# Expert weights of a two-layer transformer step: one landing buffer each for gate, up and down

## The reference

```python
gates = jnp.einsum('nk,nke->ne', g_w * top_w, jax.nn.one_hot(expert_id, N_EXPERTS, dtype=jnp.float32))
hid = jax.nn.silu(jnp.einsum('nd,edf->nef', x, w1)) * jnp.einsum('nd,edf->nef', x, w3)
out = jnp.einsum('nef,efd->nd', hid * gates[:, :, None].astype(hid.dtype), w2)
```

## Time and profile before

| | us |
|---|---|
| three runs, median | 2075.46 |
| three runs, lowest and highest | 2069.21, 2075.76 |
| the profiled execution, its own time | 2068.9 |
| its span, from first to last instruction | 2067.1 |
| its mean granted TensorE clock | 0.939 of full |

### The profile page before, as it was taken

How to read it: one execution, slowest core, us unless ns; L and a number is a source line. 1 busy time by engine, 2 the same in 40 slices (tenths; PEclk the granted TensorE clock), 3 DMA queues, 4 the chain that set the end, 5 groups by cost and what they waited for, 6 DMA issues and landing times. The chain is left out here.

```text
span 2067.1 us, 28080 instructions
## 1 busy us (share of the span) xinstructions
PE 1827.7 (88%) x11240; PEld 1513.8 (73%) x11240; DVE 1047.9 (51%) x1563; ACT 800.5 (39%) x1085; POOL 256.5 (12%) x242
## 2 busy tenths in 40 slices
PE   6799899999999996899849998989999999848892
PEld 2798555679999983677628975556799999737671
DVE  3322566762323456787672226477522334557784
ACT  2311261663112321677662203516521223227773
POOL 0101510000000000253220033100000000004430
PEclk8799999999999998899958999999999999969996
DMA  9113301312222418898762123021111225249984
GB/s 362 57 60 85 110 27 57 120 50 65 79 62 92 163 72 299 328 353 320 279 252 84 50 68 136 22 102 63 62 62 62 92 72 194 82 158 352 348 317 187
DMA packets 127958, 299.90 MB, mean 145 GB/s; under 512 B 10792, under 2 KB 53352, under 8 KB 119144
## 3 DMA queue, kind: packets, MB, share of 16 engines
q1 hardware_dynamic: 110664, 264.15, 35.2%
q0 software_dynamic: 9792, 20.99, 2.7%
q10 hardware_dynamic: 7392, 13.19, 2.2%
HBM read 283.25 MB, written 29.72 MB: 151 GB/s over the span
## 5 line engine op out<-in xcount | busy, mean ns | idle before, releaser
L1887 PE MATMUL pair<-hT_r,mid_r 128*128 128x320 f32 x768 | 237.3, 309 | 0.0
L1887 PE MATMUL pair<-mid_r,r_r 128*128 128x512 f32 (+1 forms) x528 | 193.9, 367 | 23.7 <-DVE hT_r L1679 23.6
L1887 PE MATMUL pair<-r_r,ring_r 128*128 128x320 f32 x832 | 211.8, 309 | 2.2 <-DVE ring_r L1254 2.2
L1669 DVE TENSOR_TENSOR ring_r<-ring,mid_r 128x2048 fp32r<-128x2048 f32 x68 | 155.7, 2292 | 59.1 <-ACT mid_r L1072 59.0
L1887 PE MATMUL pair<-ysT_r,mid_r 128*128 128x256 f32 (+1 forms) x768 | 172.1, 315 | 14.7 <-issue 9.5
L1887 PE MATMUL pair<-mid_r 128*128 128x320 f32 x576 | 178.9, 311 | 1.6 <-issue 1.6
L1887 PE MATMUL pair<-r_r,mid_r 128*128 128x256 f32 (+2 forms) x576 | 180.2, 313 | 0.0
L1887 PE MATMUL pair<-mid_r,ring_r 128*128 128x320 f32 x576 | 178.0, 309 | 0.0
L1969 PE MATMUL pair<-cst,mid 128*128 128x128 f32 x748 | 119.7, 300 | 64.1 <-DVE mid L1200 32.0
L1969 PEld LDWEIGHTS pair<-cst,mid 128*128 128x128 f32 x748 | 92.6, 153 | 111.3 <-DVE mid L1200 39.7
L1482 DVE TENSOR_TENSOR r<-pair,r 128x640 f32<-128x640 f32 x48 | 39.5, 823 | 252.3 <-PE pair L1887 252.3
(11 more groups left out here) (276 smaller groups left out, 3827.7 us busy)
## 6 DMA issues: line engine op xcount, KB each, us to landing
ring<-in_w_mod SPq DMA_DIRECT2D x23, 2048.0 KB, 8.8
ring<-in_w_gate SPq DMA_DIRECT2D x34, 1024.0 KB, 5.9
ring<-in_w_up SPq DMA_DIRECT2D x34, 1024.0 KB, 8.4
ring<-in_w_down SPq DMA_DIRECT2D x34, 1024.0 KB, 9.4
ring<-in_w_in SPq DMA_DIRECT2D x24, 1024.0 KB, 7.0
ring<-in_w_in SPq DMA_DIRECT2D x8, 2048.0 KB, 10.8
ring<-in_w_branch SPq DMA_DIRECT2D x12, 1024.0 KB, 5.1
ring<-in_w_out SPq DMA_DIRECT2D x8, 1024.0 KB, 5.3
```

Of the source, the lines that this page charges most:

```text
L1669: V.tensor_tensor(w13_parts[s][1][:, own], w13[s][:, own], w13_parts[s][0][:, own], ALU.subtract).then_inc(w13_ready, 1)
L1887: return nc.tensor.matmul(out, lhsT, rhs, start=first, stop=last, skip_group_check=True)
```

## The change

Three landing places take the place of four. Gate lands in 2048 columns of the ring, up in another 2048, down in 2048 columns of `hT`. Both parts of the split go elsewhere: the high parts of gate and up to `mid_r` as before, the remainders to the ring halves where they stood before; the two parts of down go to one copy each in `ysT_r`. SP issues the next load into a landing place when DVE has made the remainder from it. ACT rounds gate, down and up one after another, ahead of the hidden values, and the rounding of down(b) waits for PE's down(b-1), as its parts have one copy now. The core of the diff:

```diff
-        w13 = [view(ring, (1 - s) * 6144, 4096) for s in range(2)]
-        w2s = [view(ring, (1 - s) * 6144 + 4096, 2048) for s in range(2)]
+        gate_land, up_land, down_land = view(ring, 10240, 2048), view(ring, 4096, 2048), view(hT, 3072, 2048)
         w13_parts = [(view(mid_r, s * 4096, 4096), view(ring_r, (1 - s) * 6144, 4096)) for s in range(2)]
-        w2_parts = [(view(ysT_r, s * 2048, 2048), view(ring_r, (1 - s) * 6144 + 4096, 2048)) for s in range(2)]
+        w2_parts = view(ysT_r, 0, 2048), view(ysT_r, 2048, 2048)
...
-                    sp.wait_ge(h_filled, b + 1)
-                    for w, at_, signal in ((w_gate, 0, gate_in), (w_up, 2048, up_in)):
...
+                def load_gate(b):
 
                     e = expert_of(b)
+                    if not isinstance(b, int) or b:
+                        sp.wait_ge(gate_ready, b)
+                    load_up_part(e, w_gate, gate_land, gate_in)
...
+                def load_up(b):
 
                     e = expert_of(b)
+                    if not isinstance(b, int) or b:
+                        sp.wait_ge(up_ready, b)
+                    load_up_part(e, w_up, up_land, up_in)
+
+                def load_down(b):
+
+                    e = expert_of(b)
+                    if not isinstance(b, int) or b:
+                        sp.wait_ge(w2_ready, b)
...
-                load_up(0, 0)
-                await_job(sp, ("mod", mods_of(L) - 1))
-                load_up(1, 1)
-                load_down(0, 0)
...
+                load_gate(0)
+                load_up(0)
+                load_down(0)
+                load_gate(1)
+                load_up(1)
+                load_gate(2)
+                load_up(2)
+                load_gate(3)
+                load_down(1)
+                load_up(3)
                 with sp.Fori(0, n_more) as it:
+                    for s in range(2):
+                        load_gate(it * 2 + (4 + s))
+                        load_down(it * 2 + (2 + s))
+                        load_up(it * 2 + (4 + s))
+                for s in range(2):
+                    load_down(n_more * 2 + (2 + s))
...
+                def round_down(b):
+
+                    act.wait_ge(down_in, b * 16 + 16)
+                    act.wait_ge(y_filled, b + 2)
+                    nc.scalar.copy(w2_parts[0], down_land).then_inc(rounded, 1)
...
                     gate_values(b, s)
                     if not (last and s):
                         round_tokens(b + 1, 1 - s)
-                    round_down(s, rnd)
+                    if not last:
+                        round_gate(b + 2, s)
+                    round_down(b)
+                    if not last:
+                        round_up(b + 2, s)
                     round_hidden(b, s)
                     if not (first and s == 0):
                         store_block(b - 1, 1 - s, rnd - 1 + s)
-                    if not last:
-                        round_up(s, rnd + 1)
...
+                    if not last:
+                        remainder_gate(s, b * 5 + 7)
+                    remainder_down(b * 5 + (8 if not last else 7 if not s else 4))
+                    if last:
+                        remainder_hidden(s, b * 5 + (5 if s else 8))
+                    else:
+                        remainder_hidden(s, b * 5 + 10)
                         remainder_up(s, b * 5 + 9)
...
-                    pe.wait_ge(w13_ready, b * 2 + 2)
+                    pe.wait_ge(gate_ready, b + 1)
+                    pe.wait_ge(up_ready, b + 1)
```

More of the change, by code:

```diff
@@ L469, in bass_hybrid_step @@
         picked = [sem(f"picked{i}") for i in range(TT)]
-        gate_in = [sem(f"gate_in{i}") for i in range(2)]
-        up_in = [sem(f"up_in{i}") for i in range(2)]
-        rounded, w13_ready, w2_ready = sem("rounded"), sem("w13_ready"), sem("w2_ready")
+        gate_in, up_in = sem("gate_in"), sem("up_in")
+        rounded, gate_ready, up_ready, w2_ready = sem("rounded"), sem("gate_ready"), sem("up_ready"), sem("w2_ready")
         hid_turned, down_ready = sem("hid_turned"), sem("down_ready")
-        down_in = [sem(f"down_in{i}") for i in range(2)]
+        down_in = sem("down_in")
         t_filled, t_freed, h_filled, sil_ready, hid_ready, y_filled, y_read = (
@@ L748, in expert_of, with load_up_part @@
                     return sp.value_load(blk_ids[0:1, ds(b, 1)], min_val=0, max_val=NE - 1)
-                def load_up(b, s):
+                def load_up_part(e, w, land, signal):
+                    sp.dma_start(land, w[ds(L * NE + e, 1)].rearrange("a (p k) f -> p (a k f)", p=P)).then_inc(signal, 16)
+                def load_gate(b):
                     e = expert_of(b)
-                    sp.wait_ge(h_filled, b + 1)
-                    for w, at_, signal in ((w_gate, 0, gate_in), (w_up, 2048, up_in)):
-                        sp.dma_start(w13[s][:, at_:at_ + 2048], w[ds(L * NE + e, 1)].rearrange("a (p k) f -> p (a k f)", p=P))\
-                            .then_inc(signal[s], 16)
@@ L1066, in _, with round_gate, round_up @@
                 n_more = act.value_load(pairs_more[0:1], min_val=2, max_val=NB // 2 - 2)
[L1068 to L1077, removed]
+                def round_gate(b, s):
+                    act.wait_ge(gate_in, b * 16 + 16)
+                    nc.scalar.copy(w13_parts[s][0][:, 0:2048], gate_land).then_inc(rounded, 1)
+                def round_up(b, s):
+                    act.wait_ge(up_in, b * 16 + 16)
+                    nc.scalar.copy(w13_parts[s][0][:, 2048:4096], up_land).then_inc(rounded, 1)
+                def round_down(b):
+                    act.wait_ge(down_in, b * 16 + 16)
+                    act.wait_ge(y_filled, b + 2)
+                    nc.scalar.copy(w2_parts[0], down_land).then_inc(rounded, 1)
                 def round_tokens(b, s):
@@ L1102, in _ @@
                     act.wait_ge(h2_stored[i], 16 * ((TT + 1 - i) // 2))
+                round_gate(0, 0)
                 round_up(0, 0)
                 round_tokens(0, 0)
-                round_up(1, 0)
+                round_gate(1, 1)
+                round_up(1, 1)
                 def block_rounds(b, s, rnd, first, last):
@@ L1662, in _, with remainder_gate, remainder_down @@
                 dve.sem_inc(down_ready, 2)
+                def remainder_gate(s, count):
+                    dve.wait_ge(rounded, count)
+                    V.tensor_tensor(w13_parts[s][1][:, 0:2048], gate_land, w13_parts[s][0][:, 0:2048], ALU.subtract).then_inc(gate_ready, 1)
                 def remainder_up(s, count):
[L1666 to L1671, removed]
                     dve.wait_ge(rounded, count)
-                    V.tensor_tensor(w2_parts[s][1], w2s[s], w2_parts[s][0], ALU.subtract).then_inc(w2_ready, 1)
+                    V.tensor_tensor(w13_parts[s][1][:, 2048:4096], up_land, w13_parts[s][0][:, 2048:4096], ALU.subtract).then_inc(up_ready, 1)
+                def remainder_down(count):
+                    dve.wait_ge(rounded, count)
+                    V.tensor_tensor(w2_parts[1], down_land, w2_parts[0], ALU.subtract).then_inc(w2_ready, 1)
                 def remainder_tokens(s, count):
@@ L1692, in _ @@
                 n_more = dve.value_load(pairs_more[0:1], min_val=1, max_val=NB // 2 - 2)
-                remainder_up(0, 1)
+                remainder_gate(0, 1)
+                remainder_up(0, 2)
                 remainder_tokens(0, 3)
-                remainder_up(1, 4)
+                remainder_gate(1, 4)
+                remainder_up(1, 5)
                 def block_remainders(b, s, last):
@@ L1701, in block_remainders @@
                         remainder_tokens(1 - s, b * 5 + 6)
-                    remainder_down(s, b * 5 + (4 if last and s else 7))
-                    remainder_hidden(s, b * 5 + (5 if last and s else 8))
                     if not last:
+                        remainder_gate(s, b * 5 + 7)
[4 more added lines that the diff above has]
+                        remainder_hidden(s, b * 5 + 10)
                         remainder_up(s, b * 5 + 9)
@@ L2295, in down @@
                             last = three_products(out[:, j * 512:(j + 1) * 512], [x[:, k * P:(k + 1) * P] for x in hid_parts[s]],
-                                                  [x[:, k * D + j * 512:k * D + (j + 1) * 512] for x in w2_parts[s]], k == 0, k == FT - 1)
+                                                  [x[:, k * D + j * 512:k * D + (j + 1) * 512] for x in w2_parts], k == 0, k == FT - 1)
                     last.then_inc(y_filled, 1)
```

14 lines of the change are left out of this document (2 added, 12 removed).

## The result

The changed kernel takes 2113.84 us (median of four runs, 2110.06 to 2121.12), the kernel before, run beside it, 2072.34 us. The ratio is 1.0193, with a 95% interval from 1.0164 to 1.0223: about 40 us slower. The forecast was slower, 2083 us, and its range ended at 2103. The side was right, the forecast size a fifth of what came.

The account below looks back on a forecast made before the run. PE and the DMA engines were both taken as near their limits, neither at it. Steady part +2.3 and tails +5.5 made +7.8 us: 2068.9 became 2076.7, with the runs' median 6.6 higher 2083; range 2061 to 2103.

Parts of the forecast that it names:

- The loop: Up's single landing buffer in the experts: each block's period is the load plus 5.3 us to the next issue, 11.0 us.
- signs that I had named against myself: Profile signs against the forecast: gates 9.4 us apart, ACT waiting for gate or down, down's rounding waiting for PE, E(3) off 871.
- the steady part: Experts' blocks from E(3) to the last: 26 periods of 11.0 us, 286.0 against 283.7, so +2.3 us.
- E(3): Block 3's mark in the experts, where the sum of periods starts; claimed to stay at 871.0 us in layer 0.
- The load in it: Up's load from issue to landing: 5.7 us taken, from 4.9 to 6.6, with one gather or scatter crossing it in full.
- The tail: End of each layer's experts: PE waits 4.75 us for the last down parts, 2.76 more than before, +5.5 us in all.
- The start: First blocks of the experts: up's load for block 3 lands at 858.3 us as before, so E(3) stays at 871.0.
- The lower clock: Experts' blocks: the new kernel's lower clock costs nothing, since a slow block of 3.4 us more fits in PE's slack.
- Crowded loads: Rival, up landing buffer: gather and scatter both lie in the up load, above 6.0 us; +16 us and more, 2091 to 2106; chance 0.15.
- The clock: Rival, PE in the experts: more idling lowers the granted clock in several more blocks, +10 to +25 us; chance 0.07.
- Quiet loads: Rival, up load: meets neither gather nor scatter, 4.9 to 5.4 us; -13 to 0 us, 2062 to 2075; chance 0.27.
- the full gain: Rival, experts' blocks: ACT's load waits vanish and PE sets the period, -36 to -18 us, near 2050; chance 0.15.

Follow-up runs that it names:

- e9: The changed kernel with gather and scatter both reduced to row 0; period 10.32 us in layer 0 and 10.07 in layer 1, whole time not comparable.

## Why the prediction was wrong, step by step

**The loop** was right, in its place and its chain: I had 5.3 us from landing to the next issue, it is 5.07 and 5.01. ACT waits for up in every block from block 3 on. But three of the signs that I had named against myself came as well: waits for down (13.7 us in 9 blocks of layer 0, 16.7 us in every block of layer 1) and for gate (few in layer 0, 8 in layer 1), a rounding of down that waits for PE in the steady part (4.1 us, twice), and E(3) later (by 7.7 us, 5.6 of them from ahead of the experts). The up loop binds, but the other two stand close behind it, which the prediction had not seen.

**The load in it** was the step that failed: "5.7, which I take", and with it "L from 4.9 to 6.6". It is 7.11 and 6.98. I had put one crossing transfer (0.7) and a little of the other on top of 4.9. The experiments find both in full, 1.5 us together, and 0.67 that is left to the other weights' loads. For the loads I had written "down is issued about 4 us ahead of up and has gone by then". It had not: in the timeline above it was issued 4.8 us ahead and landed 4 us behind up's issue. When all loads take 7 us instead of 5, the loads of three loops lie on top of each other; I took each load's length as given by what the others did when they were short. The term of the sum: 26 periods of 12.0 instead of 11.0, +26 us. Another 2.9 us are in what they were compared with: I measured the old stretches from SP's gate load of block 3 to the SiLU of the last block, 283.7 us; from SiLU to SiLU they are 280.8. So the steady part, +2.3 in the sum, came out at +31.0. My own bound from above was 8.2 in the earlier trace rows, and I cut it to 6.6 without a reason from a row; with 8.2 the range would have gone to 13.5 us a block and held the result. Even my P of 11.9 makes 2106 us, and the range that I took stopped at 2103.

**The tail** was right in its mechanism, and the wait also in size. PE's last product in layer 0, then in layer 1, against the 1.99 of the earlier trace rows:

```profile
1056.30 5.49 PE L1915 MATMUL opair<-ysT_r,hT_r 128*128 128x512 f32 x12 [4.91 <-DVE hT_r L1711]
...
2076.76 5.49 PE L1915 MATMUL opair<-ysT_r,hT_r 128*128 128x512 f32 x12 [5.43 <-DVE hT_r L1711]
```

I had 4.75 (the terms written there make 4.72) for 4.91 and 5.43. The rest of +3.8 and +5.9 is the product itself: its 12 matmuls take 5.49 us in both layers, at a granted clock of 0.50, the lower of its two levels (1.2 of 2.4 GHz). The down product ahead of it took 2.88 us. In the kernel before, the last product took 4.6 us in layer 0, where the clock was already down to 0.63 in the mean, and 3.0 in layer 1 at full clock. That the longer wait would be followed by a product at the lower clock I had not priced. Nor had I seen that the last down load, issued only when the remainder before it was made, lands late too: in both layers ACT's last rounding of down waits for it (2.82 and 3.34 us), and not for the product before.

**The start** "stays at 871.0": with the delay of the first gate load from elsewhere taken off (5.6 us in layer 0), E(3) came 2.1 us later in layer 0 and 0.4 earlier in layer 1; a small term.

**The lower clock** granted for nothing: from E(3) to the last E the changed kernel had 0.95 in layer 0 and 0.98 in layer 1, against 0.95 and 0.97 before. Where its clock was lower (0.69 from 950 to 960 us), ACT still waited for the landing of up, and the chain stayed at 5.0 to 5.1 us, so it cost little in the loop.

**The rivals.** "Crowded loads" named the cause that came, with 0.15 and an end at 2106; it deserved the place of the forecast. "The clock" did not come in the steady part, only in the product of each tail. "Quiet loads" needed a load of up to 5.4 us and "the full gain" one under 4.7; the mean is 7.11, and the shortest from block 3 on 4.9. By the Trainium skill (DMA: Bandwidth & Descriptors, section on the anatomy of one DMA) an estimate for the load is 4.4 us, and a gain of 26 us; its fit is given there for transfers that GpSimd issues, and these are issued by SyncE. The trace does not agree: even without the bytes of gathers and scatters the mean was 5.57 and 5.26, and no load was under 4.7. A time for one transfer alone is no price in a loop where three share the queue.

Adding up with the measured terms: the steady part +31.0, the tails +9.7, the starts +1.7: 42.4 us of the 52.2 between the two profiled executions. The medians of the runs are 41.5 apart.

## What to carry to other kernels

A landing buffer that is free after its own use, and not after the consumer's, is gained only if there is another one to land in meanwhile: with one buffer the whole latency of the load and the whole chain behind it stand in every period (7.1 and 5.07 us here). Price such a loop with the load as it will be under the new traffic, not with the shortest of the trace. If memory does not allow a second buffer, cut the one into halves that are loaded and released each by itself; with the hidden values ahead of up's rounding, that turned +1.9% into -0.9% here, and into +0.2% in the changed kernel's own order. And look at the order behind a wait: whatever stands behind it on an engine is late too.

## What the runs showed of the hardware

About 1 us after a load was issued, the DMA engines were busy and moved little. Three neighbouring microseconds of the changed kernel, the first about 1 us after SP issued an up load at 895.45, then one after a down load at 902.01 (DMA share and GB/s are the last two numbers):

```profile
896.00:897.00 1.00, 0.59 (x4) 0.34 (x3) 1.00 (x2) 0.42 (x1) 0.91 (x1) 1.00 0.99 213
897.00:898.00 1.00, 1.00 (x6) 0.80 (x5) 1.00 (x1) 0.40 (x1) 0.99 (x2) 1.00 0.73 287
898.00:899.00 1.00, 1.00 (x6) 0.84 (x5) 0.83 (x1) 1.00 (x1) 0.87 (x1) 1.00 0.97 410
...
903.00:904.00 1.00, 1.00 (x7) 0.83 (x6) 1.00 (x2) 1.00 (x3) 0.25 (x1) 1.00 0.87 123
904.00:905.00 1.00, 1.00 (x6) 0.84 (x5) 1.00 (x1) 1.00 (x2) 1.00 (x1) 1.00 0.95 385
```

A share near one with 213 or 123 GB/s, against 410 when it flows. The same is seen where gathers and scatters move next to no bytes: in e9 SP issued an up load at 928.05, and the second and third microsecond behind it read

```profile
929.00:930.00 1.00, 0.71 (x3) 0.62 (x4) 1.00 (x2) 0.83 (x2) 1.00 (x2) 1.00 0.88 172
930.00:931.00 1.00, 1.00 (x6) 0.81 (x5) 1.00 (x1) 1.00 (x1) 1.00 (x1) 1.00 1.04 418
```

So the share is no measure of bytes: from 880 to 1000 us it is 0.87 in both kernels, at 328 and 307 GB/s. That this is the start of a queue that had run empty, and that separate issues make more such starts than pairs of gate and up did, is only argued; no run measured either by itself.
